# Layer norms of a two-block transformer kernel: sums, root and reciprocal with a token on each partition

## The reference

```python
def _rmsnorm(x, g):
    xf = x.astype(jnp.float32)
    y = xf * lax.rsqrt(jnp.mean(xf * xf, axis=-1, keepdims=True) + NORM_EPS)
    return (y * g.astype(jnp.float32)).astype(x.dtype)

def modulate(x, g, shift, scale):
    return rms_norm(x, g) * (1 + scale) + shift
...
    for l in range(DEPTH):                       # first_block
        h = _rmsnorm(x, norm_g[l])
        p = _split(h @ w_in[l])
        ...
        x = x + y @ w_out[l]
    return _rmsnorm(x, final_g)
...
    for l in range(DEPTH):                       # second_block
        h_lat = modulate(x_lat, norm_mix_g[l], sh1, sc1)
        h_ctx = modulate(x_ctx, norm_mix_g[l], csh1, csc1)
        ...  # mixer, then x_lat = x_lat + g1 * o_lat
        h_lat = modulate(x_lat, norm_ffn_g[l], sh2, sc2).reshape(B * S, D)
        ... # experts, then x_lat = x_lat + g2 * y_lat
```

## Time and profile before

| | |
|---|---|
| median of 3 runs | 1683.8 us (1681.23 to 1686.38) |
| the profiled execution: its time | 1681.12 us |
| the profiled execution: its span | 1679.5 us |
| mean granted TensorE clock | 0.951 |
| busy PE / PEld / DVE / ACT / POOL | 1539.5 / 1104.2 / 578.0 / 340.9 / 94.3 us |

### The profile page before, as it was taken

One profiled execution on the slowest core, in us unless ns is written; L12 is line 12 of the kernel. 1 busy time (PEld: TensorE's weight loads), 2 busy tenths in 40 slices (PEclk: granted clock), 3 DMA queues, 4 the chain that ended last, 5 costly groups with the idle time before them and its releaser, 6 DMA issues.

```text
span 1679.5 us, 27222 instructions
## 1 busy us (share of the span) xinstructions
PE 1539.5 (92%) x11479; PEld 1104.2 (66%) x11479; DVE 578.0 (34%) x1412; ACT 340.9 (20%) x786; POOL 94.3 (6%) x144
## 2 busy tenths in 40 slices
PE   6999899999879999998996799999869898999997
PEld 5787678877634766665535699988746575655554
DVE  2604423433345328405415011111046643233233
ACT  1313211122141123116204000000042214100010
POOL 0010000010110000002001000000010000000000
PEclk9899999999989999998997899999969998999999
DMA  8365444465872531034622799999785032999996
GB/s 267 102 204 183 144 127 135 155 198 180 212 253 88 166 126 52 26 125 131 223 80 91 262 401 392 398 400 390 308 288 187 25 126 101 381 394 386 383 387 262
DMA packets 188233, 366.95 MB, mean 218 GB/s; under 512 B 19100, under 2 KB 145912, under 8 KB 172272
## 3 DMA queue, kind: packets, MB, share of 16 engines
q1 hardware_dynamic: 171552, 322.90, 54.1%
q0 software_dynamic: 10544, 32.48, 6.1%
q10 hardware_dynamic: 6048, 10.31, 1.7%
HBM read 345.26 MB, written 20.41 MB: 218 GB/s over the span
## 4 chain that ended last, share of the span: by engine, by line
PE 80%; DVE 7%; DMA 6%; ACT 3%; issue 2%; POOL 1%; SPq 0%; POOLq 0%; ACTq 0%; DVEq 0%
PE ps_proj L646 30%; PE ps_outp L646 10%; PE ps_proj L1211 8%; PE ps_outp L1211 7%; PE ps_score L1211 7%; DMA ring<-in_exp_w 5%; PE ps_outp L1156 3%; PE ps_turn L799 2%; PE ps_outp L1311 2%; PE ps_proj L772 2%; PE ps_score L646 1%; PE ps_score L817 1%; DVE both_probs L2148 1%; DMA ring<-in_w_in 1%; PE ps_score L869 1%
## 5 line engine op out<-in xcount | busy, mean ns | idle before, releaser
L646 PE MATMUL ps_proj<-h_t,ring 128*128 128x256 f32 (+1 forms) x1280 | 358.2, 440 | 6.4 <-DMA ring<-in_w_in 2.9
L646 PEld LDWEIGHTS ps_proj<-h_t,ring 128*128 128x128 f32 x1280 | 249.2, 196 | 109.6 <-issue 76.2
L1211 PE MATMUL ps_proj<-ring,arena 128*32 128x384 f32 (+2 forms) x1760 | 117.8, 387 | 4.8 <-ACT arena L1925 2.2
L1211 PEld LDWEIGHTS ps_proj<-ring,arena 128*32 128x32 f32 (+1 forms) x1760 | 104.1, 115 | 19.1 <-issue 9.4
L1211 PE MATMUL ps_score<-ring,arena 128*32 128x384 f32 (+2 forms) x1760 | 114.6, 381 | 1.3 <-DMA ring<-in_exp_w 1.3
L1211 PE MATMUL ps_outp<-ring,arena 128*32 128x384 f32 (+2 forms) x1504 | 112.7, 417 | 3.1 <-DVE arena L2530 2.1
L1211 PEld LDWEIGHTS ps_score<-ring,arena 128*32 128x32 f32 (+1 forms) x1760 | 98.4, 113 | 16.8 <-issue 8.9
L646 PE MATMUL ps_proj<-ring,h_t 128*128 128x256 f32 (+1 forms) x512 | 105.8, 365 | 0.4 <-ACT arena L1788 0.4
L1608 ACT ACTIVATE arena<-ps_proj 128x512 f32<-128x512 f32 (+1 forms) x68 | 39.0, 576 | 314.7 <-PE ps_proj L646 313.3
L646 PEld LDWEIGHTS ps_proj<-ring,h_t 128*128 128x128 f32 x512 | 92.2, 190 | 14.8 <-issue 3.5
L1211 PEld LDWEIGHTS ps_outp<-ring,arena 128*32 128x32 f32 (+1 forms) x1504 | 81.8, 114 | 26.5 <-DVE arena L2530 3.8
(11 more groups left out here) (356 smaller groups left out, 1830.1 us busy)
## 6 DMA issues: line engine op xcount, KB each, us to landing
ring<-in_exp_w SPq DMA_DIRECT2D x138, 1024.0 KB, 11.2
ring<-in_ada_w SPq DMA_DIRECT2D x48, 1024.0 KB, 5.4
ring<-in_w_in SPq DMA_DIRECT2D x30, 1024.0 KB, 6.3
arena<-in_exp_w SPq DMA_DIRECT2D x24, 1024.0 KB, 17.5
ring<-in_even_w_in SPq DMA_DIRECT2D x12, 1024.0 KB, 6.9
ring<-in_w_out SPq DMA_DIRECT2D x8, 1024.0 KB, 5.3
row_store<-in_exp_w SPq DMA_DIRECT2D x8, 1024.0 KB, 17.1
x_t<-in_exp_w SPq DMA_DIRECT2D x16, 512.0 KB, 16.7
```

Source lines behind the costliest of these rows:

```text
L646: last = pe.matmul(out, w, a, start=(i == 0), stop=(i == len(pairs) - 1))
L1211: last = pe.matmul(b[p0:p0 + pn, c0:c0 + wn], x_of(p0, lo, pn), w(w0, wn), start=first and p0 not in strip[:i], stop=done and p0 not in st ...
```

## The change

The sums are made with the squares as the stationary operand and one column of ones moving: for each chunk and each block of 128 tokens, one matmul whose result is one PSUM column with a token on each partition. ScalarE takes the root of 128 x n/128 numbers straight from that bank; there is no copy and no second sum. VectorE takes the reciprocal of the same few numbers. TensorE then spreads them: for each block of 128 tokens, one matmul with the column of reciprocals broadcast as the stationary operand and the identity moving, into a "turn" bank. VectorE multiplies `x_t` by that bank in PSUM, not by `rstd` in SBUF, and frees the bank once its own multiplications are done (`rms_done`). TensorE waits for the reciprocal (`token_rstd_ready`) before anything that stands behind the norm in its stream. Where the norms now take a "turn" bank, the count that ScalarE waits for is named anew (`moe_latents`).

```diff
+        token_root = root[:, 1, 0:T2 // P]
+        token_rstd = rstd[:, 0:T2 // P]
...
                 base = squared[0]
                 squared[0] += 4
                 b = claim("proj")
+                norms[0] += 1
+                i = norms[0]
+                mark["token_root", i] = use["proj"]
 
                 def pairs(lo, hi):
                     for q in range(lo, hi):
                         pe.wait_ge(sq_ready, base + q + 1)
                         for k in (2 * q, 2 * q + 1):
-                            last = quarter_sum(b[:, 0:n], h[:, k, :], k)
+                            for t in range(n // P):
+                                last = pe.matmul(b[:, t:t + 1], h[:, k, t * P:(t + 1) * P], cst("ones")[:, 0:1],
+                                                 start=(k + t == 0), stop=(k + 1 == KC and t + 1 == n // P))
                     if hi == 4:
                         last.then_inc(filled["proj"], 1)
-                        sum_quarters(n)
+                        rows_of_rstd(i, n)
                 return pairs
 
-            def quarter_sum(out, sq, k):
-
-                q = 32 * (k % 4)
-                return pe.matmul(out[q:q + 32, :], cst("ones")[:, 0:32], sq, start=(k < 4), stop=(k >= 4))
-
-            def sum_quarters(n):
-
-                norms[0] += 1
-                got("proj", use["proj"])
-                b = claim("proj")
-                pe.matmul(b[:, 0:n], cst("share").to_broadcast([P, P]), root[:, 1, 0:n], start=True, stop=True
-                          ).then_inc(filled["proj"], 1)
-                mark["norm", norms[0]] = use["proj"]
+            def rows_of_rstd(i, n):
+
+                pe.wait_ge(token_rstd_ready, i)
+                b = claim("turn")
+                for t in range(n // P):
+                    last = pe.matmul(b[:, t * P:(t + 1) * P], token_rstd[:, t:t + 1].to_broadcast([P, P]), ident,
+                                     start=True, stop=True)
+                last.then_inc(filled["turn"], 1)
...
             def rms_root(n):
-                evac(root[:, 1, 0:n], n=n)
-                evac(root[:, 0, 0:n], ACT.Sqrt, n, scale=1.0 / D, bias=EPS)
+                evac(token_root[:, 0:n // P], ACT.Sqrt, n // P, scale=1.0 / D, bias=EPS)
...
                 norms[0] += 1
-                dve.wait_ge(drained["proj"], mark["norm", norms[0]])
-                for lo in range(0, n, S):
-                    cols = slice(lo, lo + S)
-                    step(dve.reciprocal(rstd[:, cols], root[:, 0, cols]))
-                    yield cols
+                dve.wait_ge(drained["proj"], mark["token_root", norms[0]])
+                dve.reciprocal(token_rstd[:, 0:n // P], token_root[:, 0:n // P]).then_inc(token_rstd_ready, 1)
+                return take("turn")
+
+            def rms_done(ready, count):
+
+                dve.wait_ge(ready, count)
+                dve.nop().then_inc(drained["turn"], 1)
...
             def normalise(h, n):
-                for cols in rms(n):
-                    x = x_t[:, :, T2 - n + cols.start:T2 - n + cols.stop]
+                rows = rms(n)
+                for lo in range(0, n, S):
+                    x = x_t[:, :, T2 - n + lo:T2 - n + lo + S]
                     for c in range(KC):
-                        dve.tensor_tensor(h[:, c, cols], x[:, c, :], rstd[:, cols], ALU.mult).then_inc(xn_ready, 1)
+                        xn[0] += 1
+                        dve.tensor_tensor(h[:, c, lo:lo + S], x[:, c, :], rows[:, lo:lo + S], ALU.mult).then_inc(xn_ready, 1)
+                rms_done(xn_ready, xn[0])
```

More of the change, by code:

```diff
@@ L387, in build @@
         xn_ready = sem("xn_ready")
+        token_rstd_ready = sem("token_rstd_ready")
         h_ready = sem("h_ready")
@@ L1524, in _ @@
                 mixed_turned(i)
+                if i == 1:
+                    mark["moe_latents", 0] = use["turn"]
             norm(h2[:, :, S:T2], S)(0, 4)
@@ L2193, in _ @@
             for l in range(DEPTH):
-                next(rms(S))
+                rows = rms(S)
                 for c in range(KC):
                     dve.scalar_tensor_tensor(out=h1[:, c, :], in0=x_t[:, c, S:T2], scalar=col_of("norm_g", l * KC + c),
-                                             in1=rstd[:, 0:S], op0=ALU.mult, op1=ALU.mult).then_inc(h_ready, 1)
+                                             in1=rows[:, 0:S], op0=ALU.mult, op1=ALU.mult).then_inc(h_ready, 1)
+                rms_done(h_ready, KC * (l + 1))
                 for i, (dst, n, lo) in enumerate(((kr_w, 160, P), (ki_w, 40, 0))):
@@ L2788, in _ @@
             add_mixed(3)
-            for cols in rms(S):
-                for c in range(KC):
-                    dve.tensor_tensor(h2[:, c, 0:S], x_t[:, c, 0:S], rstd[:, cols], ALU.mult).then_inc(xn_ready, 1)
+            rows = rms(S)
+            for c in range(KC):
+                xn[0] += 1
+                dve.tensor_tensor(h2[:, c, 0:S], x_t[:, c, 0:S], rows[:, 0:S], ALU.mult).then_inc(xn_ready, 1)
+            rms_done(xn_ready, xn[0])
             cos2 = cst("cos2").unsqueeze(1).to_broadcast([P, 2, S])
```

8 lines of the change are left out of this document (5 added, 3 removed).

## The result

The changed kernel takes 1704.3 us in the median of 5 runs (1698.5 to 1707.7), against 1686.4 for the kernel before on the same chip (1681.2 to 1690.1, 5 runs): ratio 1.0097, 95% interval 1.0073 to 1.0122. It is slower by 1%. The forecast was 1699.8 with a range of 1686 to 1709. A second measurement, `after_again`, which shares its chip and its runs of before with three of the experiments, gave 1701.2 (1696.4 to 1704.9, 6 runs), ratio 1.0112 [1.0087, 1.0138].

A forecast was written before the change was run, and what follows sets the result against it. TensorE, 80% of the last-ending chain, was taken to bound the kernel. Norm terms 2.7 + 0.3 + 5.0 + 1.0 + 5.1 + 3.1 - 1.2 = +16.0 us on the median 1683.8 gave 1699.8, range 1686 to 1709.

The forecast's parts named there:

- The clock: TensorE in the new sums: one-column passes hold 2.4 GHz no better than idle time and don't lift it from 1.2.
- first rival: All norms: the clock holds through the sums; sum -3.3 us, 1680.5, within 0.3%; chance 12%.
- price of a pass: TensorE's sums: one 128-column load per pass, 0.107 us at granted clock 1.00 and 0.21 at 0.50.
- second rival: All norms: sums are cheap, a pass below about 0.05 us; -15.4 us, 1668.4, faster by 0.9%; chance 7%.
- The tail: From last sum to first multiplication: 1.2 us in place of 3.4 for 256 tokens, 1.7 at the low clock.
- Norm 1: Program's first norm: slow sums end near 20.3, projection starts at 22.5 in place of 20.67; +2.7 us (0 to 4).
- Norm 2: First block's second layer: the gain turns into waiting for the modulation; +0.3 us (-0.3 to +2).
- Norms 3 and 4: First block's end and the 512-token norm behind, one chain: 64 passes mostly at low clock; +5.0 us (3.2 to 6.5).
- Norm 5: Ahead of the first experts, 512 tokens: 0 at full clock, up to +2.7 if it falls; +1.0 us.
- norm 8: Last experts: sum ends 0.8 later, tail 1.2 against 3.42; -1.2 us (-1.4 to +1).
- Norms 6 and 7: Second block's second layer: latents, low clock and held-up transposes, +5.1 us (4.3 to 5.9); context +3.1 (2.6 to 4.3).
- third rival: Second-layer, context and both experts' norms also drop the clock early: +25 us, 1708.8; chance 9%.

The follow-up runs named there:

- wide_sums: The changed kernel with every matmul of the token sums moving 128 columns of ones in place of one: 1680.3 us, ratio 0.9992 to the kernel before.
- wide_first_norm: The changed kernel with 128-column sums in the program's first norm only, one column in the other norms: ratio 1.0123 to the kernel before.
- wide_norms_3_4: The changed kernel with 128-column sums only in the norm ending the first block and the 512-token norm behind it: ratio 1.0085 to the kernel before.
- spread_in_outp: The changed kernel with the second block's second-layer latents' reciprocals spread into an outp bank: 1695.2 us, ratio 1.0081 to the kernel before.
- strip_sums_spread_in_outp: The changed kernel with the old sums and copy, the new small tail, and the second layer's latents' row spread into an outp bank: 1679.4 us, ratio 0.9973 to before.

## Why the prediction was right, and where it was not

**The clock.** The step that carried the forecast, that one-column sums are for the clock like idle time and don't lift it, held: it falls within dense sums (window 488 to 491), it rose inside none of the 20 low ones, and with 128 columns in the same passes the loss is gone. It held less strictly for a clock that is up: 24 one-column passes kept it in three of six second norms, and in `after_again` all 32 of the context's sums ran at full clock (3.63 us). The sum of the first rival, the clock holding through the sums, was -3.3; `wide_sums` came to 0.9992, or -1.3. That they are close says little, since the clock is low in three norms of `wide_sums` too, and comes back. The price of a pass, 0.107 at 1.00 and 0.21 at 0.50, was met: 24 passes in 2.73, 32 in 6.57, and 64 in 11.60 with the first 2.5 us at full clock. That refutes the second rival. The tail was met too: 1.21 us at full clock (from 248.34 to 249.55 in `wide_first_norm`) and 1.72 at half (253.75 to 255.47 in the changed kernel), where 1.2 and 1.7 were put. (The 96-column row on which the prediction leans there isn't among its rows; those passes, 128x96, start 0.11 apart at full clock and 0.21 at half in the trace of before.) The Trainium skill's page TensorE: Matmul & The Clock Gate, section LDWEIGHTS (loading the stationary operand), has one load time, 107 ns; the trace agrees at 1.00 and not at 0.50, where a pass took 0.205.

**Norm 1** (item 1): +2.7 was put, and the mechanism came out within 0.2: sums to 20.15 (forecast 20.3), projection at 22.57 (22.5), and its 48 passes 0.9 longer (13.15 against 12.29). The trace is 4.7 late at 104. What was missed lies at 42, where the 32 passes of 8 columns, which took 3.63 before, take 4.69, and the projection behind them slows:

```profile
42.46 4.69 PE L649 MATMUL ps_proj<-ring,h_t 128*128 128x8 f32 x32
47.00 9.43 PE L649 MATMUL ps_proj<-h_t,ring 128*128 128x256 f32 x32
```

The same 32 passes of the projection take 7.15 in `wide_first_norm`. This is old work that the change doesn't touch. I first took it for a consequence of norm 1's later end. But the projection there is slow (8.8 to 9.9) in nine of the 14 profiles, among them both versions with the old sums and both with wide sums in all norms, and it takes 7.15 in `wide_norms_3_4` and `spread_in_outp`, whose first norm has one column. So it comes and goes with the execution. What sets it stays open; the profile of before happened to be an execution without it.

**Norm 2** (item 2): the term mis-sized most: +0.3 (-0.3 to +2) was put, -0.3 to 4.3 was seen, 4.2 in both executions of the changed kernel. At full clock the working holds: in `wide_first_norm` the projection starts 0.18 later than before after 0.8 on the way in, -0.6 where -0.3 was put. The clock's drop, which I had priced as a chance at 0.6, came in five of the six executions with one-column sums there. In the changed kernel the norm cost 1.9 up to the projection (the modulation alone takes 1.7 longer) and 0.5 in it (11.05 for 10.60), and 1.7 more lie at the second of the old narrow places above, which the forecast didn't have.

**Norms 3 and 4** (item 3): +5.0 (3.2 to 6.5) was put; the first multiplication came 5.3 later than the kernel was late on the way in (10.3 at 466, 15.6 at 485), against 4.8 forecast (489.6 for 484.80). The 64 passes were partly at full clock, as I had taken them; less those 10.3 they end at 487.4, where 487 was put. That is in part luck: I had taken the clock as low from 475, as before, and in fact it was low in the modulation ahead and up again (0.98) when the sums began. Another 1.7 went between 493 and 597: it is the third of the old narrow places, 10.03 against 8.36.

**Norm 5** (item 4) was put at +1.0 and its stretch gave -0.8; **norm 8** (item 7) was put at -1.2 and gave -0.9. Norm 5 itself gave nothing: its first multiplication came 1.7 later (0.3 forecast), ScalarE's shift took that back, as forecast, and what was gained came only behind it, between 912 and 1124 (-1.4), among the experts. **Norms 6 and 7** (items 5 and 6) were put at 8.2 and gave 10.9. The first multiplication of the latents' norm, +2.9 by the forecast, came at +2.3, the split transposes came as described (the wait of 2.03 above), and the projection came at +4.9 (5.5 forecast). Up to the context's sums it is +4.1, a microsecond under the 5.1 put for item 5; item 6, put at 3.1, is what was mis-sized, with 5.5 up to the slot behind the next (all counted from 17.0 late at 1229). What exceeds is the context's sums, 4.76 in place of the 3.43 plus 0.25 put down, its spread, 1.22 for 0.45, and what follows at the same clock, which fell once more here (8.48 for the 32 passes of the next slot, 7.07 before). In `after_again` it did not fall in these sums.

The window over them, then the timeline:

```profile
1275.00:1279.00 4.00, 4.00 (x30) 0.75 1.01 428
```

```profile
1274.75 4.76 PE L702 MATMUL ps_proj<-const,h_t 128*128 128x1 f32 x32
...
1279.98 1.22 PE L714 MATMUL ps_turn<-const,rstd 128*128 128x128 f32 x4 [0.46 <-DVE rstd L2129]
```

**The sum.** +16.0 was put. The trace ends 26.6 late, while the ratios say 16.4 (0.0097 of 1686) and 19 (0.0112 of 1682). The profiled execution was as long as the longest of the five, and that of before (1681.12) shorter than any of the five beside it, so that the difference of the two is too large for the median. Of the 10.6 by which the trace exceeds the forecast about half lies at the three old narrow places (2.0 by 104, 1.7 and 1.7). So it is in part luck that the medians differ by 17.9, within 2 us of the 16.0: in the trace items 1, 2, 3 and 6 were put too low by 2 to 4 us each, items 4 and 5 too high by 1 to 2, and how much of that holds for the median no run shows.

The third rival, the clock lost everywhere, was right for norms 2 and 7. In 5 and 8 the clock did fall inside the sums:

```profile
896.00:899.00 3.00, 3.00 (x25) 0.86 0.97 387
899.00:902.00 3.00, 2.52 (x12) 0.50 0.05 6
```

But there it had the price wrong. What follows waits for ScalarE, and TensorE's clock was at 0.50 behind these norms before as well:

```profile
885.00:890.00 5.00, 0.37 (x1) 0.50 0.01 2
1400.00:1405.00 5.00, 4.23 (x16) 0.50 0.00 0
```

With its 1708.8 it was nearer to the profiled execution (1707.7), the forecast nearer to the median.

**Tails.** The forecast said that a shorter tail turns into waiting for the modulation or the transposes. In the second norm of `strip_sums_spread_in_outp`, where the clock stays up and the modulation takes 1.93, the projection comes neither earlier nor later than the kernel was on the way in (4.8 both times), though the tail is 1 us shorter: that gain is waited away. For the transposes the three pairs above show it. The two ratios, 0.9997 without and 0.9973 with the freed bank, point the same way, but their intervals overlap.

## What to carry to other kernels

Moving a reduction onto partitions shortens what other engines do with it, but on TensorE it turns few long matmuls into many loads with one column behind each. Look up the granted clock where the profile has such narrow passes, and count what follows them at the lower level too, since here the sums themselves grew by 32 us (11.5 and 6.8 for the two forms of L704 before, 50.4 now) off and on the path while the time at 0.50 grew by 57. If narrow passes can't be avoided, try moving columns that nobody needs: here 128 columns in place of one made the kernel 1.2% faster, while 32 left it slow (1.0070). And before spreading a result into a bank, see who else waits for that bank.

## What the runs showed of the hardware

- At granted clock 1.00, 24 passes with a 128x128 load each take 2.73 us with one column behind every load and 2.84 with 128: the load sets the price. At 0.50 a pass takes about 0.2 with 1 or 128 columns.
- The clock, once at 0.50, rose inside none of 20 dense sums of 32 or 64 one-column passes, and inside all 9 that moved 128 columns. An up clock fell inside sums of one column and, in the norm of 512 tokens, of 128.
- The mean granted clock ordered these three kernels as their times: 0.935 and 1704 for one column, 0.950 and 1693 for 32, 0.960 and 1680 for 128. It is no gauge across different ones: the kernel before has 0.951 and 1684.
- The clock row isn't always right at the start of the program. In `wide_sums` the window below says 1.00, but 16 passes took 3 us, the price of 0.50; in `wide_first_norm` 28 passes ran in the same window. Other kernels here show the same. The duration of a known pass is the surer gauge.

```profile
14.00:17.00 3.00, 3.00 (x16) 1.00 1.03 370
```

- Executions of one kernel differ by 11 us in `wide_first_norm` (1695 to 1707) and by 14 in the kernel before (1674 to 1688). Where the traces of different kernels share the same work, they differ at places of narrow passes: the 16-column ones took 8.36 to 10.76. One profile of before and one of after can't tell a term of 4 us at such a place from chance.
